# Attention scores from each head's own 32 or 64 partitions, without GpSimd's masked copies of the queries

## The chip, the cores and the metric

The kernel runs on one core of a Trainium2 chip. The metric is the device time of one execution in microseconds, as the median of several. The engines are TensorE (PE in rows of the profile, PEld for its weight loads), VectorE (DVE), ScalarE (ACT), GpSimd (POOL) and SyncE (SP, which only issues DMAs here). SBUF has 128 partitions; a matmul contracts over partitions and writes PSUM, which has eight banks.

## The reference

Two blocks in float32. The first has two layers on 256 latent tokens and 256 context tokens of width 1024: token mixers in four groups (spatial gating A, Fourier mixing B, differential attention C, neighbourhood attention D), then a mixture of 16 experts; the second has feed-forward layers, a recurrent unit and pooling, and is not touched here. What matters is in C and D:

```python
q, k: (tokens, 4 heads, 2 maps, 32)          # group C, normed, rope
s = einsum('bqhmd,bkhmd->bhmqk', q, k) * 32 ** -0.5
a = softmax(s); w = a[:, :, 0] - lam * a[:, :, 1]
out_c = einsum('bhqk,bkhd->bqhd', w, v)
q, k: (tokens, 4 heads, 64)                  # group D, normed
s = q . k * 64 ** -0.5 + bias(-inf outside the window), context keys without bias
out_d = softmax(s) v
```

So a score of C is a product over 32 numbers and one of D over 64.

## The kernel before

One program for five engines, each with its own order of instructions written out by hand and ordered among each other by semaphores. Per layer the mixers run as: input projections (`projection`), transposes of queries and keys of C (`turn_qk(l, 0)`), spatial gating, Fourier, attention C (`attention_c`), transposes of D (`turn_qk(l, 1)`), attention D (`attention_d`), `merge`, then routing and the experts. In layer 0 only, `ada_group` steps (L709, L717: a product of `ada_w` with the conditioning, on four 32-column strips of TensorE, then transposes) stand between these on TensorE.

`qk_t` holds the transposed queries (blocks 0 and 1) and keys (blocks 2 and 3), 128 features on the partitions and tokens along the free dimension. In C a block has two heads with two maps of 32 features each, in D two heads of 64. A full product over 128 partitions would mix these. So GpSimd writes copies of the queries in which all partitions but the head's own are zero (L496 for C, L513 for D: a multiplication by a 0/1 column of `const`, `band_c`, `band_d`) into `q_band`, and TensorE takes the product of that copy with the whole block of keys (L819, L857).

A unit is one query tile of 128 tokens and one head: 16 in layer 0 (four tiles), 8 in layer 1. `keys(q)` gives 512 keys for latent tiles (the first eight units) and 256 for context tiles (the other eight of layer 0). Every engine takes the units in turn. In C, PE in iteration u: four (or two) transposes of the weights of u (L832) into bank 6, the two score products of u + 3 (L819) into banks 2(u % 3) and the next, then the value product of u (L841). VectorE: the weights of u + 1 in four steps (L1775, L1776, L1778 and L1779, the last reads two tensors in SBUF and writes one), then the two maxima of u + 3 (L1763, read from PSUM), and at each new tile a copy of the finished tile (L1768); the next tile's value product waits for that copy, and so does all behind it on PE. ScalarE: the copy of the turned weights (L1346) and the exponentials (L1335). The exponentials of u + 3 free the bank pair.

In D, PE in iteration u: the score of u + 2 (L857), for latent tiles followed by a product that adds the bias `rel_bias` (L861), the transposes of u + 1 (L871), the value product of u (L886). ScalarE has there, besides exponentials (L1359) and copies (L1377), squares and roots for the norm of the outputs, with a table load at each change, and a piece of `w_out` (L354).

GpSimd in a layer, strictly in this order: DMAs of `att` (Fourier tables and the mask) and `rel_bias`, the 8 copies of the first four C units, two more each time a unit's scores are done, the addition of the mask to `rel_bias` (L505, 128 x 2048, SBUF to SBUF), the D copies. PE's `attention_d` waits once for `bias_ready`, which L505 gives. The weights of all stages come by DMA through a ring of six slots of 2 MB; SyncE issues a load when PE has released the slot (`weights_used`).

Of the kernel before, what the change touches and what calls it, by code (L numbers as in the profile page):

```python
# [19 lines left out]
ALU = mybir.AluOpType  # L20
# [3 lines left out]
P = 128  # L24
# [7 lines left out]
HEADS, HEAD = 4, 64  # L32
# [29 lines left out]
CONST = {"ident": P, "slot_row": CAP, "slot_col": 1, "band_c": P // DIFF, "band_d": P // HEAD, "cos": 4 * DIFF, "sin": 4 * DIFF}  # L62
# [15 lines left out]
def lru_pairs():  # L78
# [18 lines left out]
    "c_bands": 16, "d_bands": 16, "c_scores": 32, "c_max": 32, "c_exp": 32, "c_weights": 16, "c_turned": 16, "c_wt": 16, "c_pv": 16, "c_out": 4,  # L97
# [29 lines left out]
def build(nc, dram, out_t):  # L127
    ctx = ExitStack()
    with ctx:
# [5 lines left out]
        def sem(name):  # L135
            if name not in sems:
                sems[name] = ctx.enter_context(nc.semaphore(name))
            return sems[name]
# [30 lines left out]
        def part(lo, hi):  # L169
            return arena[:, lo:hi]  # L170
# [7 lines left out]
        q_band = part(7168, 8192).rearrange("p (b f) -> p b f", b=8)  # L178
# [290 lines left out]
        def _(pool):  # L469
            for l in range(LAYERS):  # L470
# [15 lines left out]
                pool.wait_ge(sem("qk_t_act"), 1 + before("qk_t_act", l))  # L486
                pool.wait_ge(sem("qk_t_dve"), 1 + before("qk_t_dve", l))
                band = const[:, columns(CONST, "band_c")]
                for u, (q, h) in enumerate(units(l)):
                    if u == 0:  # L490
                        pool.wait_ge(sem("qk_turned"), 4 + before("qk_turned", l))
                    if u >= 4:
                        pool.wait_ge(sem("c_scores"), 2 * (u - 3) + before("c_scores", l))
                    for m in range(2):
                        g = 2 * h + m
                        ins = pool.tensor_scalar(q_band[:, 2 * (u % 4) + m, :], qk_t[:, g // 4, P * q:P * q + P],  # L496
                                                 band[:, g % 4:g % 4 + 1], None, ALU.mult)
                    ins.then_inc(sem("c_bands"), 1)

# [6 lines left out]
                pool.wait_ge(sem("qk_t_act"), 3 + before("qk_t_act", l))  # L506
                pool.wait_ge(sem("qk_t_dve"), 3 + before("qk_t_dve", l))
                pool.wait_ge(sem("c_scores"), 2 * len(units(l)) + before("c_scores", l))
                band = const[:, columns(CONST, "band_d")]
                for u, (q, h) in enumerate(units(l)):  # L510
                    if u >= 8:
                        pool.wait_ge(sem("d_scores"), u - 7 + before("d_scores", l))
                    pool.tensor_scalar(q_band[:, u % 8, :], qk_t[:, h // 2, P * q:P * q + P],  # L513
                                       band[:, h % 2:h % 2 + 1], None, ALU.mult).then_inc(sem("d_bands"), 1)
# [154 lines left out]
        def _(pe):  # L669
# [134 lines left out]
            def attention_c(l):  # L804
# [4 lines left out]
                def scores(u):  # L809
# [7 lines left out]
                    pe.wait_ge(sem("c_bands"), u + 1 + before("c_bands", l))  # L817
                    for m in range(2):
                        pe.matmul(ps[:, 2 * (u % 3) + m, 0:width], q_band[:, 2 * (u % 4) + m, :],  # L819
                                  qk_t[:, 2 + (2 * h + m) // 4, lo:lo + width], start=True, stop=True)\  # L820
                            .then_inc(sem("c_scores"), 1)
# [23 lines left out]
            def attention_d(l):  # L845
# [5 lines left out]
                def scores(u):  # L851
                    q, h = todo[u]
                    lo, width = keys(q)
                    if u >= 3:
                        pe.wait_ge(sem("d_exp"), u - 2 + before("d_exp", l))
                    pe.wait_ge(sem("d_bands"), u + 1 + before("d_bands", l))
                    mm = pe.matmul(ps[:, u % 3, 0:width], q_band[:, u % 8, :], qk_t[:, 2 + h // 2, lo:lo + width],  # L857
                                   start=True, stop=q >= 2)
# [1368 lines left out]
def host_constants():  # L2227
# [9 lines left out]
    const["band_c"] = np.kron(np.eye(P // DIFF), np.ones((DIFF, 1)))  # L2237
# [144 lines left out]
```

## Time and profile before

| | us |
|---|---|
| three executions | 2664.91, 2666.49, 2666.72 |
| median | 2666.49 |
| profiled execution | 2663.66 |
| its span, first to last instruction | 2661.9 |
| busy in it: TensorE, VectorE, ScalarE, GpSimd | 2294.2, 1036.2, 810.8, 67.6 |
| mean granted clock of TensorE | 0.967 of full speed |
| DMA: moved, mean rate | 660.17 MB, 248 GB/s |
| layer 0: C from about 179 to 230, D from 242 to 286 | |
| layer 1: C from about 996 to 1034, D from 1037 to 1068 | |

Times in rows are from the start of the span. In the chain of waits each piece lasts from its start until the next piece could begin; in the timeline a row is a group of like instructions, whose durations overlap where TensorE is pipelined, so starts are the safer numbers.
### The profile page before, as it was taken

The page shows a single profiled execution, that of the slowest core. Times are in us where ns is not written, and L with a number is a line of the kernel's source. Part 1 is how long each engine was busy: PE and PEld are TensorE (multiplying, and loading weights), DVE is VectorE, ACT ScalarE, POOL GpSimd, SP SyncE. Part 2 cuts the span into 40 slices and gives each one's busy share as a digit, 9 for nine tenths or more (in the row PEclk, how much of TensorE's full clock was granted, in tenths as well). Part 3 has the DMA queues.
Part 4 walks back from the last instruction along what each step waited for, and adds up shares of the span by engine and source line. Part 5 has one row for each costly group of instructions (what it writes and reads, how often), then busy time and mean ns, then how long its engine had stood idle before and what let it go on. Part 6 is the DMA issues. An engine that isn't in the chain of part 4 may idle for free.

```text
span 2661.9 us, 32502 instructions
## 1 busy us (share of the span) xinstructions
PE 2294.2 (86%) x13947; PEld 1607.4 (60%) x13952; DVE 1036.2 (39%) x1361; ACT 810.8 (30%) x989; POOL 67.6 (3%) x99
## 2 busy tenths in 40 slices
PE   5998888877777897797777779999999989979997
PEld 3855643222222685531111129998999989978997
DVE  4536451000000556410000005557765565555555
ACT  3425321100000346310000004434644354334433
POOL 0023000000000002000000000000000000010000
PEclk8999899999999998799999999999999999999998
DMA  6292256999999230479999993444354434442441
GB/s 269 111 382 120 118 217 281 428 428 429 428 427 429 101 138 0 180 310 428 429 428 428 429 428 157 189 162 175 127 190 184 157 149 186 189 158 97 188 174 68
DMA packets 49840, 660.17 MB, mean 248 GB/s; under 512 B 5616, under 2 KB 7152, under 8 KB 8144
## 3 DMA queue, kind: packets, MB, share of 16 engines
q1 hardware_dynamic: 48640, 653.67, 60.0%
q0 software_dynamic: 1104, 5.11, 0.5%
q8 instruction: 73, 1.20, 0.2%
q14 instruction: 23, 0.19, 0.0%
HBM read 657.71 MB, written 1.05 MB: 247 GB/s over the span
## 4 chain that ended last, share of the span: by engine, by line
PE 58%; DMA 29%; DVE 7%; ACT 4%; issue 1%; SPq 0%; POOL 0%; DVEq 0%; ACTq 0%; POOLq 0%
DMA ring<-in_exp_down 13%; PE ps L680 13%; PE ps L681 13%; PE ps L682 13%; DMA ring<-in_exp_gate 12%; PE ps L997 4%; PE ps L1012 3%; DMA ring<-in_ffn_w 2%; DVE ring_r L361 2%; PE ps L553 2%; ACT ring_r L354 1%; PE ps L1028 1%; PE ps L819 1%; DMA ring<-in_w_in 1%; PE ps L964 1%
## 5 line engine op out<-in xcount | busy, mean ns | idle before, releaser
L997 PE MATMUL ps<-ring,arena 128*64 128x512 f32 (+1 forms) x2048 | 468.3, 602 | 136.2 <-DMA ring<-in_exp_up 64.8
L680 PE MATMUL ps<-h_buf_r,ring_r 128*128 128x256 f32 (+1 forms) x1856 | 539.8, 291 | 16.5 <-DVE h_buf_r L638 12.2
L682 PE MATMUL ps<-h_buf_r,ring_r 128*128 128x256 f32 (+1 forms) x1856 | 537.2, 289 | 0.0
L361 DVE TENSOR_TENSOR ring_r<-ring,ring_r 128x4096 fp32r<-128x4096 f32 (+2 forms) x97 | 406.1, 4192 | 301.3 <-ACT ring_r L354 301.3
L681 PE MATMUL ps<-h_buf_r,ring_r 128*128 128x256 f32 x1696 | 483.0, 285 | 0.0
L997 PEld LDWEIGHTS ps<-ring,arena 128*64 128x64 f32 (+1 forms) x2048 | 129.6, 124 | 473.6 <-issue 294.3
L354 ACT ACTIVATE ring_r<-ring 128x4096 fp32r<-128x4096 f32 (+2 forms) x97 | 332.7, 3434 | 255.1 <-DMA ring<-in_ffn_w 226.4
L680 PEld LDWEIGHTS ps<-h_buf_r,ring_r 128*128 128x128 f32 x1856 | 359.6, 194 | 21.7 <-issue 16.8
L682 PEld LDWEIGHTS ps<-h_buf_r,ring_r 128*128 128x128 f32 x1856 | 359.5, 194 | 3.1
L681 PEld LDWEIGHTS ps<-h_buf_r,ring_r 128*128 128x128 f32 x1696 | 328.5, 194 | 0.2
L681 PE MATMUL ps<-arena_r,ring_r 128*128 128x256 f32 (+1 forms) x944 | 277.8, 294 | 0.0
L1012 PE MATMUL ps<-ring,arena 128*64 128x512 f32 (+1 forms) x1024 | 232.2, 597 | 32.3 <-ACT arena L1444 19.8
L1954 DVE TENSOR_TENSOR arena<-arena,ps 128x512 f32<-128x512 f32 (+1 forms) x32 | 21.9, 683 | 560.9 <-PE ps L997 560.9
L680 PE MATMUL ps<-arena_r,ring_r 128*128 128x256 f32 x784 | 223.5, 285 | 3.4 <-DVE arena_r L1988 1.8
L682 PE MATMUL ps<-arena_r,ring_r 128*128 128x256 f32 x784 | 222.9, 284 | 0.0
L681 PEld LDWEIGHTS ps<-arena_r,ring_r 128*128 128x128 f32 x944 | 182.6, 193 | 3.1
L1012 PEld LDWEIGHTS ps<-ring,arena 128*64 128x64 f32 (+1 forms) x1024 | 62.0, 123 | 181.4 <-issue 118.1
L680 PEld LDWEIGHTS ps<-arena_r,ring_r 128*128 128x128 f32 x784 | 151.5, 193 | 4.5 <-DVE arena_r L1988 2.3
L682 PEld LDWEIGHTS ps<-arena_r,ring_r 128*128 128x128 f32 x784 | 151.5, 193 | 0.0
L1962 DVE COPY arena<-ps 32x512 f32 x32 | 21.9, 686 | 285.9 <-PE ps L1012 285.9
L1444 ACT ACTIVATE arena<-ps 128x512 f32<-128x512 f32 (+1 forms) x32 | 15.7, 490 | 322.8 <-PE ps L1004 322.8
L680 PE MATMUL ps<-ring_r,h_buf_r 128*128 128x512 f32 (+1 forms) x240 | 92.5, 386 | 15.3 <-DVE arena_r L619 15.3
(273 smaller groups left out, 2311.5 us busy)
## 6 DMA issues: line engine op xcount, KB each, us to landing
ring<-in_exp_gate SPq DMA_DIRECT2D x64, 2048.0 KB, 25.4
ring<-in_exp_up SPq DMA_DIRECT2D x64, 2048.0 KB, 25.6
ring<-in_exp_down SPq DMA_DIRECT2D x64, 2048.0 KB, 24.9
ring<-in_ffn_w SPq DMA_DIRECT2D x60, 2048.0 KB, 8.2
ring<-in_ada_w SPq DMA_DIRECT2D x24, 2048.0 KB, 15.2
ring<-in_w_in SPq DMA_DIRECT2D x6, 2048.0 KB, 19.1
ring<-in_ffn_w SPq DMA_DIRECT2D x12, 1024.0 KB, 4.9
ring<-in_lru_w SPq DMA_DIRECT2D x6, 2048.0 KB, 8.3
```

Source lines behind the costliest of these rows:

```text
L354: act.activation(halves(n)[0][:, 0:halved[n]], slot(n)[:, 0:halved[n]], ACT.Copy).then_inc(sem("chunk_lead"), 1)
L361: dve.tensor_tensor(rest, slot(n)[:, 0:halved[n]], lead, ALU.subtract).then_inc(sem("chunk_halved"), 1)
L553: mm = pe.matmul(ps[:, 0, 0:width], mean_w[:, :], squares(i)[:, k, 0:width], start=k == 0, stop=k == KT - 1)
L680: release(pe.matmul(out, a[0], b[0], start=start, stop=False, skip_group_check=True))
L681: pe.matmul(out, a[0], b[1], start=False, stop=False, skip_group_check=True)
L682: return pe.matmul(out, a[1], b[0], start=False, stop=stop, skip_group_check=True)
L819: pe.matmul(ps[:, 2 * (u % 3) + m, 0:width], q_band[:, 2 * (u % 4) + m, :], qk_t[:, 2 + (2 * h + m) // 4, lo:lo + width], start=True, stop ...
L964: mm = pe.matmul(ps[:, j % 6, :], h, one_hot, start=a == 0 and i == 0, stop=a == 1 and i == 1)
L997: mm = pe.matmul(ps[half * m:half * m + m, which, :], xe[:, k, :], slot(n + c)[:, D * (k % 4) + 512 * half:D * (k % 4) + 512 * half + 512] ...
L1012: mm = pe.matmul(ps[half * m:half * m + m, 3, :], hid_t[:, k % 4, k // 4, :], slot(n + c)[:, D * (k % 4) + 512 * half:D * (k % 4) + 512 * ...
L1028: mm = pe.matmul(ps[:, 4 + d % 4, N * s:N * s + N], o[:, g, P * d:P * d + P], scatter[:, s, g, :], start=g == 0, stop=g == 3)
L1954: dve.tensor_tensor(hid, hid, ps[0:2 * m, 1, :], ALU.mult).then_inc(sem("exp_hid"), 1)
```

## The change

Scores read only the head's own partitions: for C the strip `32*(2*(h%2)+m)` to +32 of block `h//2` of the queries and of block `2 + h//2` of the keys, for D the strip `64*(h%2)` to +64. TensorE addresses such a product to the same rows of its array (32x128 at row 0, 32, 64 or 96; 64x128 at row 0 or 64). The two maps of a C unit are on two neighbouring strips, the next head's on the other two. All of GpSimd's copies, their waits, semaphores, buffer and constants are gone. Banks, the order on the other engines and the values computed stay.

```diff
@@ GpSimd, per layer
                 pool.dma_start(rel_bias, dram["rel_bias"][l]).then_inc(sem("rel_bias_loaded"), 16)
 
-                pool.wait_ge(sem("qk_t_act"), 1 + before("qk_t_act", l))
-                pool.wait_ge(sem("qk_t_dve"), 1 + before("qk_t_dve", l))
-                band = const[:, columns(CONST, "band_c")]
-                for u, (q, h) in enumerate(units(l)):
-                    if u == 0:
-                        pool.wait_ge(sem("qk_turned"), 4 + before("qk_turned", l))
-                    if u >= 4:
-                        pool.wait_ge(sem("c_scores"), 2 * (u - 3) + before("c_scores", l))
-                    for m in range(2):
-                        g = 2 * h + m
-                        ins = pool.tensor_scalar(q_band[:, 2 * (u % 4) + m, :], qk_t[:, g // 4, P * q:P * q + P],
-                                                 band[:, g % 4:g % 4 + 1], None, ALU.mult)
-                    ins.then_inc(sem("c_bands"), 1)
-
                 pool.wait_ge(sem("att_loaded"), 16 + before("att_loaded", l))
                 pool.wait_ge(sem("rel_bias_loaded"), 16 + before("rel_bias_loaded", l))
...
                 pool.tensor_tensor(biases, biases, masks, ALU.add).then_inc(sem("bias_ready"), 1)
-                pool.wait_ge(sem("qk_t_act"), 3 + before("qk_t_act", l))
-                pool.wait_ge(sem("qk_t_dve"), 3 + before("qk_t_dve", l))
-                pool.wait_ge(sem("c_scores"), 2 * len(units(l)) + before("c_scores", l))
-                band = const[:, columns(CONST, "band_d")]
-                for u, (q, h) in enumerate(units(l)):
-                    if u >= 8:
-                        pool.wait_ge(sem("d_scores"), u - 7 + before("d_scores", l))
-                    pool.tensor_scalar(q_band[:, u % 8, :], qk_t[:, h // 2, P * q:P * q + P],
-                                       band[:, h % 2:h % 2 + 1], None, ALU.mult).then_inc(sem("d_bands"), 1)
@@ TensorE, attention_c, scores(u)
-                    pe.wait_ge(sem("c_bands"), u + 1 + before("c_bands", l))
                     for m in range(2):
-                        pe.matmul(ps[:, 2 * (u % 3) + m, 0:width], q_band[:, 2 * (u % 4) + m, :],
-                                  qk_t[:, 2 + (2 * h + m) // 4, lo:lo + width], start=True, stop=True)\
-                            .then_inc(sem("c_scores"), 1)
+                        b, own = h // 2, slice(DIFF * (2 * (h % 2) + m), DIFF * (2 * (h % 2) + m) + DIFF)
+                        pe.matmul(ps[:, 2 * (u % 3) + m, 0:width], qk_t[own, b, P * q:P * q + P],
+                                  qk_t[own, 2 + b, lo:lo + width], start=True, stop=True).then_inc(sem("c_scores"), 1)
@@ TensorE, attention_d, scores(u)
-                    pe.wait_ge(sem("d_bands"), u + 1 + before("d_bands", l))
-                    mm = pe.matmul(ps[:, u % 3, 0:width], q_band[:, u % 8, :], qk_t[:, 2 + h // 2, lo:lo + width],
-                                   start=True, stop=q >= 2)
+                    own = slice(HEAD * (h % 2), HEAD * (h % 2) + HEAD)
+                    mm = pe.matmul(ps[:, u % 3, 0:width], qk_t[own, h // 2, P * q:P * q + P],
+                                   qk_t[own, 2 + h // 2, lo:lo + width], start=True, stop=q >= 2)
```

Where GpSimd's instructions stand. Before, layer 0, from the load of `rel_bias` on (L496 C copies, L505 the mask addition, L513 D copies; lines are those of the kernel before):

```order
L484 DMA h_buf<-in_rel_bias 128x2048
L496 ISA
L496 TENSOR_SCALAR arena<-arena,const 128x128 [waits qk_turned,qk_t_dve,qk_t_act]
L496 TENSOR_SCALAR arena<-arena,const 128x128 x7
L496 TENSOR_SCALAR arena<-arena,const 128x128 [waits c_scores]
...
L505 TENSOR_TENSOR h_buf<-h_buf 128x2048 [waits rel_bias_loaded,att_loaded]
L513 TENSOR_SCALAR arena<-arena,const 128x128 [waits c_scores,qk_t_dve,qk_t_act]
L513 TENSOR_SCALAR arena<-arena,const 128x128 x7
L513 TENSOR_SCALAR arena<-arena,const 128x128 [waits d_scores] x8
```

After the change, GpSimd in layer 0 and on to layer 1 (line numbers are those of the changed kernel: L490 is the mask addition, L481 to L483 the three loads):

```order
L482 DMA h_buf<-in_att 128x1280
L483 DMA h_buf<-in_rel_bias 128x2048
L490 ISA
L490 TENSOR_TENSOR h_buf<-h_buf 128x2048 [waits rel_bias_loaded,att_loaded]
L476 DMA rows<-in_rows 128x384 [waits moe_added,sgu_done,qk_ready]
L477 DMA arena<-in_sgu_t 128x512
L481 DMA h_buf<-in_att 128x256 [waits proj_done]
```

The mask addition L505 stood behind 32 C copies, of which 24 (in pairs, the first of a pair) wait for `c_scores`; as L490 it stands behind the loads and waits for them alone.

TensorE at the start of stretch C in layer 0, before (L819 scores, L832 transposes, L841 value product):

```order
L819 MATMUL ps<-arena 128x512 [waits c_bands,qk_t_dve,qk_t_act]
L819 MATMUL ps<-arena 128x512
L819 MATMUL ps<-arena 128x512 [waits c_bands]
L819 MATMUL ps<-arena 128x512
L819 MATMUL ps<-arena 128x512 [waits c_bands,fourier_read]
L819 MATMUL ps<-arena 128x512
L832 MATMUL ps<-const,arena 128x128 [waits c_weights]
L832 MATMUL ps<-const,arena 128x128 x3
L819 MATMUL ps<-arena 128x512 [waits c_bands,c_exp]
L819 MATMUL ps<-arena 128x512
L841 MATMUL ps<-arena 128x64 [waits c_wt]
```

and in the changed kernel (L795 scores, L807 transposes, L816 value product):

```order
L795 MATMUL ps<-arena 128x512 [waits qk_t_dve,qk_t_act]
L795 MATMUL ps<-arena 128x512 x3
L795 MATMUL ps<-arena 128x512 [waits fourier_read]
L795 MATMUL ps<-arena 128x512
L807 MATMUL ps<-const,arena 128x128 [waits c_weights]
L807 MATMUL ps<-const,arena 128x128 x3
L795 MATMUL ps<-arena 128x512 [waits c_exp]
L795 MATMUL ps<-arena 128x512
L816 MATMUL ps<-arena 128x64 [waits c_wt]
L816 MATMUL ps<-arena 128x64 x3
L807 MATMUL ps<-const,arena 128x128 [waits c_wt,c_weights]
```

No instruction of TensorE has moved; the waits for `c_bands` are gone, and with them the only link from GpSimd to stretch C.

## Rows read from the trace of the kernel before

**Rows 1.** Chain of waits, layer 0, one steady unit: start us, us, engine and line.
```profile
193.34 0.44 PE ps L832 x4
193.78 1.72 PE ps L819 x4
195.50 0.84 PE ps L841 x8
```

**Rows 2.** Timeline, VectorE: start us, us, engine, line, operation, names, shapes, count [idle].
```profile
1013.76 1.27 DVE L1763 TENSOR_REDUCE small<-ps 128x1 f32<-128x512 f32 x2
1014.96 0.15 DVE L1775 RECIPROCAL small<-small 128x2 f32<-128x2 f32 x1
1016.53 0.68 DVE L1763 TENSOR_REDUCE small<-ps 128x1 f32<-128x512 f32 x1
...
217.59 0.74 DVE L1763 TENSOR_REDUCE small<-ps 128x1 f32<-128x256 f32 x2
218.26 0.15 DVE L1775 RECIPROCAL small<-small 128x2 f32<-128x2 f32 x1
219.43 0.75 DVE L1763 TENSOR_REDUCE small<-ps 128x1 f32<-128x256 f32 x2
```

**Rows 3.** Line L1779 (min/median/max ns); timeline: L1779 in layer 1, L505.
```profile
L1779 DVE SCALAR_TENSOR_TENSOR arena<-arena,small x16: 483/751/4608, 186.3 to 227.0; 128x512 f32<-128x512 f32 x8, 128x256 f32<-128x256 f32 x8
...
1008.96 4.88 DVE L1779 SCALAR_TENSOR_TENSOR arena<-arena,small 128x512 f32<-128x512 f32 x1
...
212.82 4.56 POOL L505 TENSOR_TENSOR h_buf<-h_buf 128x2048 f32<-128x2048 f32 x1
```

**Rows 4.** GpSimd's queue in the timeline, and DMA issues of two stretches.
```profile
149.01 0.54 POOL L484 DMA_DIRECT2D h_buf<-in_rel_bias  x1
...
h_buf<-in_rel_bias POOLq DMA_DIRECT2D x1, 1024.0 KB, 17.4
...
988.21 0.54 POOL L484 DMA_DIRECT2D h_buf<-in_rel_bias  x1
...
h_buf<-in_rel_bias POOLq DMA_DIRECT2D x1, 1024.0 KB, 6.4
```

**Rows 5.** Timeline, VectorE: the first maximum of each layer's stretch C.
```profile
180.52 1.48 DVE L1763 TENSOR_REDUCE small<-ps 128x1 f32<-128x512 f32 x2 [0.55 <-PE ps L819]
...
997.07 0.69 DVE L1763 TENSOR_REDUCE small<-ps 128x1 f32<-128x512 f32 x1 [0.17 <-PE ps L819]
```

**Rows 6.** Timeline, TensorE: full tiles, then 128x32 column strips (L709), twice.
```profile
150.15 1.89 PE L788 MATMUL ps<-arena 128*128 128x256 f32 x8
...
151.98 7.07 PE L709 MATMUL ps<-ring,cond 128*32 128x512 f32 x64
...
163.72 7.07 PE L776 MATMUL ps<-arena,h_buf 128*128 128x256 f32 x32
...
170.72 5.36 PE L709 MATMUL ps<-ring,cond 128*32 128x512 f32 x48
```

**Rows 7.** Timeline, VectorE: the copies L1768 that the counts end at.
```profile
224.73 0.41 DVE L1768 COPY arena<-ps 128x256 f32<-128x256 f32 x1
...
1024.59 0.41 DVE L1768 COPY arena<-ps 128x256 f32<-128x256 f32 x1
```

**Rows 8.** Window (busy us of PE, PEld, DVE, ACT, POOL; clock; DMA), timeline.
```profile
1004.00:1009.00 5.00, 5.00 (x21) 3.22 (x20) 3.42 (x8) 2.15 (x5) 1.55 (x3) 0.66 0.00 0
...
1004.23 3.12 PE L819 MATMUL ps<-arena 128*128 128x512 f32 x4
```

**Rows 9.** Window, layer 0, stretch D (columns as in rows 8).
```profile
242.00:286.00 44.00, 35.94 (x200) 26.94 (x202) 27.14 (x68) 31.36 (x61) 4.82 (x8) 0.88 0.22 93
```

**Rows 10.** Timeline, layer 1: last copy ahead of stretch D, its first score.
```profile
1035.93 0.69 DVE L1753 COPY arena<-ps 128x512 f32<-128x512 f32 x1 [1.00 <-PE ps L799]
...
1036.83 1.10 PE L857 MATMUL ps<-arena 128*128 128x512 f32 x2 [0.94 <-POOL arena L513]
```

**Rows 11.** Waits of the DMA queue: us in total, times, longest.
```profile
SPq L440 <- PE ps L997: 561.5, 120, 44.3
```

More of the change, by code:

```diff
@@ L60 @@
 ROWS_W = sum(ROWS.values())
-CONST = {"ident": P, "slot_row": CAP, "slot_col": 1, "band_c": P // DIFF, "band_d": P // HEAD, "cos": 4 * DIFF, "sin": 4 * DIFF}
+CONST = {"ident": P, "slot_row": CAP, "slot_col": 1, "cos": 4 * DIFF, "sin": 4 * DIFF}
 CONST_W = sum(CONST.values())
@@ L96 @@
     "fourier_uv": 4, "uv_ready": 4, "fourier_done": 4, "fourier_read": 2,
-    "c_bands": 16, "d_bands": 16, "c_scores": 32, "c_max": 32, "c_exp": 32, "c_weights": 16, "c_turned": 16, "c_wt": 16, "c_pv": 16, "c_out": 4,
+    "c_scores": 32, "c_max": 32, "c_exp": 32, "c_weights": 16, "c_turned": 16, "c_wt": 16, "c_pv": 16, "c_out": 4,
     "d_scores": 16, "d_max": 16, "d_exp": 16, "d_turned": 16, "d_wt": 16, "d_pv": 16, "d_out": 16,
@@ L177, in build @@
         expo = part(4096, 7168).rearrange("p (b f) -> p b f", b=6)
-        q_band = part(7168, 8192).rearrange("p (b f) -> p b f", b=8)
         qk_d = part(8192, 10240).rearrange("p (t f) -> p t f", t=4)
@@ L2235, in host_constants @@
     }
-    const["band_c"] = np.kron(np.eye(P // DIFF), np.ones((DIFF, 1)))
-    const["band_d"] = np.kron(np.eye(P // HEAD), np.ones((HEAD, 1)))
     half = DIFF // 2
```

## The prediction

> **What bounds the kernel now.** Outside the two attention stretches nothing in the kernel is touched, so I read those, one per layer, and first the chain of waits there. In layer 0's first attention (the "C" heads, `attention_c`) the chain lies on TensorE: per unit (one head of one query tile, 512 keys) four transposes 0.44 us, the two score products 1.72, the eight passes of the value product 0.84, together 3.00 [rows 1]. GpSimd's copies are nowhere in it. Then VectorE, at two places where score results lay ready: from the first of a unit's two maxima to the first step of the weights 1013.76 to 1014.96, 1.20 us, and on to the next unit's maxima at 1016.53, so 1.57 for the four steps of weights and 2.77 in all. With 256 keys the same rows give 0.67, 1.17 and 1.84 [rows 2]. **VectorE is only 0.23 us per unit behind TensorE: it is the next bound, and it caps what shorter scores can give.** Third, the longest single item on either chain: the step L1779 takes 0.483 or 0.751 us, but once per layer 4.61 and 4.88, when GpSimd's addition of the mask (L505, 4.56 us) is running [rows 3]. The order of GpSimd's program puts L505 behind all the copies of stretch C, so it falls into the middle of VectorE's work.
>
> **Part 1: the mask addition moves.** With no copies ahead of it, L505 starts when its loads land: in layer 0 149.01 + 17.4 = 166.4 us, in layer 1 988.21 + 6.4 = 994.6 [rows 4]. It then runs until about 171.0 and 999.2. In layer 0 the first maximum is taken at 180.52: cover enough [rows 4, 5]. In layer 1 VectorE does one copy out of PSUM and maxima over PSUM from 997.07 on, and its first step on two SBUF tensors comes after 1002 [rows 5]. I take nothing for a collision there; the upper bound is what L505 still has to run at 996.2, 3.0 us (a rival below). Gain: 4.61 − 0.48 = 4.13 and 4.88 − 0.75 = 4.13, **8.3 us**, both on the chain. The Trainium skill ("SBUF — State Buffer", section "SBUF: two separate sides") says that GpSimd and a VectorE operation with two SBUF inputs exclude each other for the whole instruction; the long L1779 agrees with it, and so does taking nothing for operations that read PSUM.
>
> **Part 2: scores in row tiles.** Each product is two passes of 512 columns, 0.43 us each [rows 1]. Fewer rows do not shorten a pass (I assume; it streams as many columns), so the gain can only be overlap. The two products of a unit now use different 32-row strips and different PSUM banks. The trace has no row strips side by side, but column strips: 64 passes L709 on 128x32 strips, 512 wide, take 7.07 us, 0.11 each against 0.43 of a score pass, so four ran at once [rows 6, 1]. Bounds: no overlap (1.72 per unit) and full overlap of a pair (0.86). I take 0.86, since the nearest row shows overlap between strips for the same type and width.
>
> **Part 3: changes of tile shape.** TensorE now changes between 128 rows and 32 or 64 rows twice per unit. Price: L788's 8 passes to L709 are 1.83 us, L776's 32 passes of the same width to L709 7.00; the 24 between them cost 5.17, 0.2155 each, which leaves 0.105 for the change [rows 6]. Two per unit are 0.2 us; bounds 0 (hidden) and 0.2. TensorE's unit in stretch C becomes 3.00 − 0.86 + 0.2 = 2.34, under VectorE's 2.77: the changes are hidden and **VectorE is the bound.**
>
> **Part 4: stretch C anew, by VectorE's clock.** The maxima of the first three units no longer wait for passes of 0.86 us each. I count from the first maximum (180.52; 997.07) to the copy L1768 that gates the last value products (224.73 in layer 0, ahead of unit 12's; 1024.59 in layer 1, ahead of unit 4's) [rows 5, 7]. Behind that copy only transposes, value products and ScalarE copies follow, unchanged.
> Layer 0: maxima of 8 units at 1.20 and 8 at 0.67 = 14.96; weights of units 0 to 13, 8 x 1.57 + 6 x 1.17 = 19.58; two earlier copies at about 0.33; sum 35.2, so 215.7. Layer 1: 8 x 1.20 + 6 x 1.57 = 19.0, so 1016.1.
> New waits: (a) TensorE ends the first scores about 0.6 us after the first maximum begins, and the first weights end 3 x 1.20 + 1.57 after it, so TensorE now idles some 4.5 us. Before, in layer 1, the pause in this place was followed by 5 us at a granted 0.66 of full speed, part of them at 1.2 GHz, and the four score passes took 3.12 us there [rows 8]. I expect one such stretch at 1.2 GHz at each start: transposes 0.88 and scores 1.72 instead of 0.44 and 0.86, against VectorE's 1.57 of cover: 2.6 + 0.3 − 1.57 = 1.3 us per layer (bounds 0 and 3). (b) Where a new query tile begins, the copy, value product, transposes and scores run in series: 0.41 + 0.84 + 0.44 + 0.43 (two passes of 256) + 0.2 + some 0.3 of hand-overs = 2.6 us, against VectorE's own 0.33 + 1.57: it waits 0.7. At the next, with 256 keys in all of it, 0.41 + 0.42 + 0.22 + 0.43 + 0.2 + 0.3 = 2.0 against 1.5: 0.5. Both lie inside layer 0's count, none in layer 1's.
> Copy L1768 at 215.7 + 1.3 + 1.2 = 218.2 instead of 224.73: **−6.5 us**. Layer 1: 1016.1 + 1.3 = 1017.4 instead of 1024.59: **−7.2 us**. Part 1 is contained in both.
>
> **Part 5: the second attention ("D").** One product per unit, nothing beside it to overlap with, so no gain in scores. The chain names GpSimd's copies once, at layer 1's first D score (0.94 us), but the copy L1753 of the transposed keys ends at 1035.93 + 0.69 = 1036.62 and the score starts at 1036.83 [rows 10]: the real wait is for VectorE, gain 0. In layer 0 `ada_group` lies ahead. The cost is 24 units x 0.2 = 4.8 us of shape changes. In layer 0's D neither engine is busy throughout (TensorE 35.94 and ScalarE 31.36 of 44 us [rows 9]), now one is late and now the other, so I take half, **+2.4 us** (bounds 0 and 4.8).
>
> **What follows later.** Stretches behind are chains of engines, and the expert weights are requested when TensorE frees a slot (120 waits, 561.5 us [rows 11]), so the experts' DMA-bound part starts earlier by the same amount and keeps its length. GpSimd's other work is not in any chain.
>
> **Sum.** −6.5 − 7.2 + 2.4 = −11.3 us. The profiled execution took 2663.66 (span 2661.9), 2.83 under the median of the three runs, 2666.49; the change of 11.3 is set against both alike: 2652.4 profiled, **2655.2 us** as a median. A difference under 0.2% (5.3 us) can't be told from none.
>
> **Rivals.**
> (A) *No overlap of row strips.* TensorE stays the bound with 3.00 + 0.2 per unit. Of the count 13 and 5 units pay 0.2; 8.3 − 3.6 − 2.4 = 2.3 us gained: 2664. For: no row shows row strips side by side. Against: L709 [rows 6]. Chance 0.10.
> (A') *Passes start strictly in program order.* The two passes of one product sit on one strip, one behind the other; then a pair takes three steps, 1.29 us, a unit 3.00 − 0.43 + 0.2 = 2.77, level with VectorE, and each of the four waits of part 4 grows by 0.43: 2655.2 + 1.7 = 2656.9. For: the trace has no row of it. Against: L709 also has two passes per product and strip, and runs four at once. Chance 0.05. The Trainium skill ("TensorE: Matmul & The Clock Gate", section "The mechanism" of its part 3) states this rule: matmuls start and end in program order.
> (B) *Slower: the granted clock stays low.* TensorE now pauses in every unit and fills 32 of 128 rows; if 1.2 GHz holds through stretch C, a unit is 0.88 + 1.72 + 1.68 + 0.2 = 4.5 us against 3.00. Layer 0: 8 x 1.5 + 8 x 0.3; layer 1: 8 x 1.5 less the 3 us that its low stretches cost already; + 2.4 of D, − 8.3: about +17, 2684. It decides against the change once more than six or seven 512-key units run low (each 4.5 − 2.77 = 1.7 us against 11.3). For: rows 8. Against: low stretches there lasted one or two units. Chance 0.06.
> (C) *The mask addition collides elsewhere.* Layer 1's first copy and maxima wait until 999.2, 3 us: 2658. For: rows 3. Against: those read PSUM. Chance 0.10.
> (D) *Half the gain is lost later*, to falls of the clock at new places (in one such stretch four score passes stood at 3.12 us [rows 8], which are 1.72 of the chain elsewhere) or to a transfer: 2661. Chance 0.07.
> My forecast has 0.62.
>
> **How the numbers follow.** Fast end: no low clock at the starts (−2.6) and shape changes hidden (−2.4) and low stretches of before gone (−2): 2648. Slow end: A, 2664. B alone lies outside, with parts of A. Faster by over 0.2%, below 2661.2: the forecast, A', C, and part of D: 0.80. Slower: B, 0.05. Same: the rest, 0.15.
>
> **What would show it.** Score passes that start in pairs, about 0.86 us per unit; VectorE without idle in stretch C, unit to unit 2.8 us; L1779 never above 0.8; L505 at 166 and 995 us; D units about 0.2 longer where TensorE is late. Score passes at 1.72 per unit mean A; a granted clock near 0.5 across stretch C means B; a copy L1746 of 3 us means C. Wrong beyond the range: a gain above 18 us, which would need VectorE to be shorter than counted.

## The result, and the profile after

The changed kernel took **2696.76 us** (median of 2692.03, 2695.79, 2697.74 and 2702.26), against 2666.6 us of the kernel before on the same chip: a ratio of 1.0115, 95% interval 1.0095 to 1.0135. It is 30 us **slower**, where 11 us less was forecast. Its runs spread over 10 us, those of before over 2. The profiled execution took 2692.03 us, with a span of 2690.2.

Start with TensorE's clock in the attention stretches of the changed kernel. The view is the table by windows, with the granted clock in the column PEclk; the first four windows are in layer 0 and the last two in layer 1.

```profile
core 0: us, PE busy (x) PEld busy (x) DVE busy (x) ACT busy (x) POOL busy (x), PEclk, DMA share, GB/s
180.60:185.40 4.80, 0.79 (x4) 0.00 (x0) 4.65 (x10) 3.98 (x10) 0.00 (x0) 1.00 0.97 410
185.40:250.20 64.80, 58.51 (x220) 38.73 (x224) 34.64 (x93) 25.70 (x76) 0.00 (x0) 0.50 0.28 120
250.20:284.40 34.20, 31.47 (x186) 17.35 (x178) 16.60 (x42) 22.54 (x40) 0.00 (x0) 1.00 0.45 184
284.40:311.70 27.30, 25.60 (x95) 16.30 (x98) 10.74 (x28) 9.55 (x23) 0.00 (x0) 0.50 0.04 9
1021.10:1025.10 4.00, 0.86 (x7) 0.04 (x2) 3.91 (x8) 3.18 (x6) 1.88 (x1) 1.00 0.00 0
1025.10:1066.00 40.90, 35.12 (x128) 24.31 (x128) 19.68 (x44) 15.23 (x38) 0.00 (x0) 0.50 0.00 0
```

In layer 0 the clock is at 1.2 GHz (0.50) for 65 us without a break, all of stretch C, and for 27 us more from near the end of stretch D on; in layer 1 for 41 us. The same view of the kernel before has a mean of 0.94 over its stretch C of layer 0 (180.5 to 233 us) and 0.87 over that of layer 1 (997 to 1036): dips of a few us each.

The timeline of TensorE at the start of stretch C in layer 0, changed kernel (L795 scores, L807 transposes, L816 value product; they answer to L819, L832 and L841 in [rows 1]):

```profile
179.41 1.99 PE L795 MATMUL ps<-arena 32*128 32x512 f32 x12
...
185.95 1.11 PE L807 MATMUL ps<-const,arena 128*128 128x128 f32 x4 [4.56 <-DVE arena L1754]
186.99 2.08 PE L795 MATMUL ps<-arena 32*128 32x512 f32 x4
189.00 1.97 PE L816 MATMUL ps<-arena 128*128 128x64 f32 x8
190.76 1.06 PE L807 MATMUL ps<-const,arena 128*128 128x128 f32 x4
...
195.52 1.06 PE L807 MATMUL ps<-const,arena 128*128 128x128 f32 x4
```

Three things are to be seen. Twelve score passes start and end within 1.99 us, where before they took 5.32: strips overlap. Then TensorE idles 4.56 us. From there a unit lasts 190.76 − 185.95 = 4.81 us and then 195.52 − 190.76 = 4.76, TensorE has no gap in it, and every pass takes about twice as long as at full clock. VectorE, which was to be the bound, waits in each unit (timeline of VectorE, changed kernel):

```profile
193.86 1.29 DVE L1738 TENSOR_REDUCE small<-ps 128x1 f32<-128x512 f32 x2 [1.89 <-PE ps L795]
```

The mask addition did what was expected. It starts at 166.49 us, and the step that it used to delay (L1754, formerly L1779) has no long case left (timeline of GpSimd, and groups by shape of VectorE in stretch C of layer 0, to set beside [rows 3]):

```profile
166.49 4.51 POOL L490 TENSOR_TENSOR h_buf<-h_buf 128x2048 f32<-128x2048 f32 x1 [17.03 <-DMA h_buf<-in_rel_bias]
```
```profile
L1754 DVE SCALAR_TENSOR_TENSOR arena<-arena,small 128x512 f32<-128x512 f32 x8 | 6.0, 751 | 0.3
```

And the two copies that the prediction used as marks, L1743 now, beside the first maxima of their stretch (timeline of VectorE; the first two rows are layer 0, the others layer 1):

```profile
180.64 3.68 DVE L1738 TENSOR_REDUCE small<-ps 128x1 f32<-128x512 f32 x6 [0.74 <-PE ps L795]
...
237.67 0.41 DVE L1743 COPY arena<-ps 128x256 f32<-128x256 f32 x1
...
1021.14 3.68 DVE L1738 TENSOR_REDUCE small<-ps 128x1 f32<-128x512 f32 x6 [0.36 <-PE ps L795]
...
1049.85 0.42 DVE L1743 COPY arena<-ps 128x256 f32<-128x256 f32 x1
```

From first maximum to copy, layer 0 took 57.0 us (before 44.2, forecast 37.7) and layer 1 28.7 (before 27.5, forecast 20.3) [rows 5, 7]. Layer 1's stretch begins 24.1 us later than before, so most of the loss (28.3 us by the spans) had been made in layer 0 by then. Of these 24.1 us, 16.2 had been lost when stretch D began (first score of D at 257.82 us, before at 241.58) and 5.0 more within stretch D (48.9 us from its first score to the next `ada_group`, before 43.9). In layer 1 the same two steps are 5.5 and 1.1 us.

One execution of the kernel with strips in stretch C alone (3021 us, below) was disturbed and stands outside all comparisons.

### The profile page after: what moved, and what is told of

It reads as the page before. It is cut to its first block, busy times and chain, and to the rows that moved or that the text cites. A ratio compares the mean times of both kernels' runs of the same rounds, so it can differ in the third digit from the quotient of the medians.

```text
span 2690.2 us, 32387 instructions
## 1 busy us (share of the span) xinstructions
PE 2330.7 (87%) x13947; PEld 1622.4 (60%) x13952; DVE 1026.7 (38%) x1361; ACT 811.2 (30%) x989; POOL 24.7 (1%) x27
## 4 chain that ended last, share of the span: by engine, by line
PE 59%; DMA 29%; DVE 6%; ACT 4%; issue 1%; SPq 0%; DVEq 0%; ACTq 0%
DMA ring<-in_exp_down 13%; PE ps L656 13%; PE ps L657 13%; PE ps L658 13%; DMA ring<-in_exp_gate 12%; PE ps L972 4%; PE ps L987 3%; PE ps L529 2%; DVE ring_r L360 2%; DMA ring<-in_ffn_w 2%; PE ps L816 1%; PE ps L1003 1%; ACT ring_r L353 1%; PE ps L795 1%; DMA ring<-in_w_in 1%; PE ps L685 1%
## 5 line engine op out<-in xcount | busy, mean ns | idle before, releaser
L1419 ACT ACTIVATE arena<-ps 128x512 f32<-128x512 f32 (+1 forms) x32 | 15.7, 491 | 322.9 <-PE ps L979 322.9
## 6 DMA issues: line engine op xcount, KB each, us to landing
ring<-in_ada_w SPq DMA_DIRECT2D x24, 2048.0 KB, 15.2
```

## Experiments

Two questions: which half of the change brings the loss, and what holds the clock down. Theory R (in some expectations S, S2 or, in its last form, H): the strip passes do (they use 32 or 64 of 128 rows). Rival P: the longer pause does. In the diffs, `filler(n)` issues n products of `qk_t[:, 0, 0:P]` with `qk_t[:, 2, 0:N]` (full rows, 256 columns) into a PSUM bank that nobody reads then.

### The mask addition alone, and each half alone

First, the kernel before with the mask addition ahead of all query copies.

```diff
...
+                pool.tensor_tensor(biases, biases, masks, ALU.add).then_inc(sem("bias_ready"), 1)
                 for u, (q, h) in enumerate(units(l)):
...
-                pool.tensor_tensor(biases, biases, masks, ALU.add).then_inc(sem("bias_ready"), 1)
```

> The kernel before with one edit: GpSimd adds the mask to rel_bias ahead of its query copies for stretch C, not behind them. All passes stay on full rows. Theory T (part 1 of the prediction): VectorE's L1779, which waited for the shared port in stretch C, loses its long outliers, 4.1 us a layer, so about 8.3 us less than before, near 2658 us, and the granted clock stays as it was. Rival: GpSimd's first copies now start behind the addition (4.6 us), and the first scores of stretch C wait for them, so that the gain is given back: 2662 to 2671 us.

Measured: 2664.42 us against 2667.35, ratio 0.9984 (0.9975 to 0.9993), so about 4 us less by the ratio. Both were right in part. No long L1779 is left (eight at 751 ns, eight at 484 in layer 0). But in layer 1 the first copies now stood behind the addition, and TensorE waited for them (groups by shape, 985 to 1037 us):

```profile
L819 PE MATMUL ps<-arena 128*128 128x512 f32 x32 | 18.0, 703 | 4.6 <-POOL arena L502 4.6
```

Then the strips in stretch C alone (D keeps its copies), and in stretch D alone (C keeps its copies, the addition behind them). The edits are the two halves of the change; the kernel with strips in C alone has the moved mask addition too.

> Only stretch C reads strips of 32 partitions; stretch D keeps GpSimd's masked copies and full rows. In the changed kernel the landmarks fell back by some 16 us in stretch C of layer 0, some 7 us in stretch D of layer 0 and some 6 us in layer 1. If the loss belongs to the 32-row passes of stretch C (theory S: while they run, the granted clock stays at 0.5), this kernel keeps the 22 us of stretch C and is 18 to 26 us slower than before, with the clock at 0.5 from about 185 to 230 us. If the 64-row passes of stretch D are to blame as much as those of C, it is 10 to 15 us slower. If the loss needs both, under 5 us.

> Only stretch D reads strips of 64 partitions; stretch C keeps GpSimd's masked copies and full rows, and the mask addition stays behind them. Theory S2 (64-row passes lower the granted clock too, in proportion to rows in use): the clock falls to 0.5 in stretch D and the kernel is 5 to 9 us slower than before. Rival (the low clock in stretch D of the changed kernel was an effect of what C left behind, or of the times at which ada_group 4 fell): the clock stays near that of before, and the time is within 0 to +3 us of before (part 5 of the prediction said +2.4).

Measured: C alone 2684.14 us, ratio 1.0057 (1.0042 to 1.0073); D alone 2684.86, ratio 1.0059 (1.0039 to 1.0080). By the ratios the halves cost 15.2 and 15.7 us, together as much as the change (0.0057 + 0.0059 against 0.0115). That fits the case of halves that are to blame alike, where 10 to 15 us had been expected of C alone; theory S had 18 to 26 for it, and theory S2 5 to 9 for D alone. C alone includes what the moved addition gives, so its strips cost more than 15.2. The equal sums do not show that the changed kernel loses half in D: in its profiled execution, the fastest of four, the two stretches D were 5.0 and 1.1 us longer than before, in that of D alone, the second slowest of five, 13.4 and 11.4. The profile of C alone was taken again:

> The kernel with strips in stretch C alone once more, for its profile: the first one was of a disturbed execution (3021 us, the whole of it at 0.75). Theory R: the clock is at 0.5 from about 185 us to the end of stretch C, and in stretch D as in the kernel before. Rival (the low clock of stretch D in the changed kernel came from stretch C): nothing to see in D here or in the kernel with strips in D alone, which has shown 48 us of it.

This one took 2683.2 us (by windows, layer 0: stretch C, then from its end to the middle of stretch D):

```profile
185.00:249.00 64.00, 57.65 (x216) 38.54 (x220) 34.49 (x93) 25.73 (x76) 1.37 (x3) 0.50 0.28 119
250.00:286.00 36.00, 30.12 (x196) 19.17 (x188) 17.75 (x46) 26.18 (x43) 7.10 (x12) 1.00 0.43 175
```

D alone, by windows and by TensorE's timeline where the clock falls:

```profile
243.60:256.70 13.10, 12.28 (x53) 6.70 (x53) 5.56 (x13) 8.85 (x16) 0.00 (x0) 1.00 0.79 340
256.70:304.50 47.80, 46.84 (x160) 32.50 (x164) 21.86 (x57) 22.93 (x46) 0.00 (x0) 0.50 0.00 1
1058.80:1106.60 47.80, 43.72 (x139) 31.01 (x138) 21.07 (x47) 29.34 (x48) 0.00 (x0) 0.50 0.00 1
```
```profile
256.64 1.11 PE L861 MATMUL ps<-const,arena 128*128 128x128 f32 x4 [0.82 <-ACT arena L1349]
```

Strips in C lower the clock in C and leave D as it was; strips in D lower it in D, in both layers. As it was does not mean 1.0 throughout: the kernel before, full rows in every score, has a low stretch of 10.2 us in its own stretch D of layer 0 (window below, kernel before), where TensorE waited up to 2.6 us for ScalarE, and C alone has one of 10.2 us at the same units.

```profile
271.00:281.00 10.00, 7.41 (x30) 6.12 (x28) 6.56 (x13) 2.86 (x10) 0.00 (x0) 0.50 0.00 0
```

In D alone, from 243.6 us to the fall, TensorE waited once, 0.82 us; in the kernel before it waited 0.37 and 1.50 us in the same place and the clock stayed up. A long pause is not needed.

### The pause

> The changed kernel with nine full-row passes of 256 columns, whose results nobody reads, right behind the first three units' scores, where TensorE idled 4.56 us. Theory P (the pause brings the clock down, and it then stays down): without the pause the clock stays at 1.0 through most of stretch C, and the time falls by 15 us or more against the changed kernel, to about 2680 or less. Theory S (the 32-row passes themselves): the clock falls again within some units, as no full-row passes come between, and the time stays above 2690.

```diff
                 for u in range(3):
                     scores(u)
+                filler(9)
```

Measured: 2680.54 us, ratio 1.0052 (1.0036 to 1.0067) where the changed kernel has 1.0115: about half of the loss is gone, as P said. But the profile shows what R said too: the clock holds for five units and falls behind the next pause, 1.93 us long.

```profile
190.82 1.10 PE L821 MATMUL ps<-arena 128*128 128x64 f32 x8 [0.26 <-ACT arena L1326]
...
193.60 1.10 PE L821 MATMUL ps<-arena 128*128 128x64 f32 x8 [0.17 <-ACT arena L1326]
...
200.91 1.08 PE L821 MATMUL ps<-arena 128*128 128x64 f32 x8 [1.93 <-DVE arena L1748]
```
```profile
203.10:237.20 34.10, 30.14 (x121) 21.98 (x122) 17.83 (x56) 12.83 (x43) 0.00 (x0) 0.50 0.02 10
```

While it held, a unit took 193.60 − 190.82 = 2.78 us, with VectorE never idle: the pace that part 4 had worked out (2.77).

> The changed kernel with the nine full-row passes behind the first scores and one more full-row pass of 256 columns at the end of each unit of stretch C (0.43 us at full clock). With the first nine alone the clock fell at 203 us, not at 185, and the kernel was 13 us slower than before. Theory R (strip passes, which use part of the rows, do not keep the clock up, full-row passes do): the clock stays at 1.0 in stretch C of layer 0, the units take 2.8 us, stretch D still falls as it did, and the time is 2672 to 2678. Rival (it is the idle time, of which little is left): no further change, 2680.

```diff
+                filler(9)
...
                     mm.then_inc(sem("c_pv"), 1)
+                    filler(1)
```

Measured: 2687.97 us (eight runs, 2680.98 to 2703.89), ratio 1.0083 (1.0058 to 1.0109). Neither theory's figure, and a spread of 23 us. In layer 1 the clock held through all of stretch C; in layer 0 it fell behind a pause of 1.80 us at 200 us, and the full-row product of 256 columns in each unit did not bring it back:

```profile
200.30:251.50 51.20, 47.18 (x168) 33.69 (x172) 19.93 (x60) 14.78 (x47) 0.00 (x0) 0.50 0.05 19
...
1030.00:1084.00 54.00, 45.47 (x246) 29.92 (x244) 32.98 (x71) 34.98 (x68) 1.88 (x1) 1.00 0.00 1
```

Now the pause without strips. VectorE gets four more maxima over SBUF ahead of its first weights:

```diff
+                for i in range(4):
+                    dve.tensor_reduce(d_max[:, i:i + 1], qk_t[:, 0, :], AX, ALU.max)
                 weights(0)
```

> The kernel before, all passes on full rows, with four extra maxima of 512 columns on VectorE ahead of its first unit of each stretch C (they read SBUF and nobody uses what they give), so that TensorE's first pause grows from 2.4 to about 4.8 us, as in the changed kernel. Rival P (the pause alone brings the clock down for long): the clock falls to 0.5 near 185 us and stays there for tens of us, and the time rises by 10 us or more. Theory R (strips): one dip of 3.4 us, and 2 x 2.4 us plus the dips: 2672 to 2675.

Measured, one execution: 2671.07 us beside 2667.74 of before, 1 us under what theory R had. The pause is 4.73 us, longer than the changed kernel's 4.56, and the dip is 6.8 us, twice the expected 3.4. By the timeline, and by windows:

```profile
188.41 1.11 PE L832 MATMUL ps<-const,arena 128*128 128x128 f32 x4 [4.73 <-DVE arena L1779]
```
```profile
186.50:193.30 6.80, 4.89 (x12) 2.83 (x12) 4.24 (x11) 1.38 (x3) 0.26 (x1) 0.50 1.01 429
```

**Behind the same pause the clock is low for 6.8 us with full rows, and for 65 us with strips.** P alone falls: the low stretch starts at the pause, and what follows decides how long it lasts.

### Rows and the clock, without any wait

Blocks of passes that wait for nobody, put ahead of stretch C of layer 0. For n rows on the strips that start at r:

```diff
+                    for i in range(count):
+                        r = starts[i % len(starts)]
+                        pe.matmul(ps[:, r // 32, 0:N], qk_t[r:r + n, 0, 0:P], qk_t[r:r + n, 2, 0:N], start=True, stop=True)
```

> The kernel before with blocks of TensorE passes of 128x256 whose results nobody reads, ahead of stretch C of layer 0, one behind the other without a wait: full rows (20 us) before and after each of: 64 rows; 32 rows; 32 rows on two strips in turn; 32 rows on four strips in turn; 64 rows on two strips in turn. Theory R: with 64 or 32 rows of one strip the clock falls to 0.5 inside the block and comes back in the full-row block behind it; with strips in turn that overlap to cover all 128 rows it stays at 1.0, and two strips of 32 behave as 64 rows do. Rival (rows do not matter, only idle time): the clock stays at 1.0 through all blocks, since TensorE never waits. The overlap: a pass of 256 columns takes 0.43 us alone, 0.22 on two strips in turn, 0.11 on four.

By windows: 64 rows; 32 rows; full rows again; 32 rows on two strips; on four strips; 64 rows on two strips.

```profile
202.00:229.00 27.00, 27.00 (x126) 23.20 (x125) 0.00 (x0) 0.00 (x0) 0.00 (x0) 1.00 0.07 28
...
254.00:301.00 47.00, 47.00 (x111) 36.57 (x111) 0.00 (x0) 0.00 (x0) 0.00 (x0) 0.50 0.00 0
305.00:323.00 18.00, 18.00 (x85) 15.86 (x84) 0.00 (x0) 0.00 (x0) 0.00 (x0) 1.00 0.00 1
325.00:351.00 26.00, 26.00 (x244) 23.10 (x242) 0.00 (x0) 0.00 (x0) 0.00 (x0) 1.00 0.01 1
373.00:400.00 27.00, 27.00 (x504) 25.64 (x504) 0.00 (x0) 0.00 (x0) 0.00 (x0) 1.00 0.01 2
422.00:449.00 27.00, 27.00 (x254) 24.23 (x252) 0.00 (x0) 0.00 (x0) 0.00 (x0) 1.00 0.01 1
```

TensorE is busy in all of every window. With 32 rows of one strip the clock fell 3.4 us into the block and came back in the full-row block, so "idle time alone" falls. That 64 rows of one strip held it at 1.0 was not as R expected. The overlap is complete (timeline of TensorE; 64 rows, then 32 rows on two strips and on four):

```profile
201.29 27.89 PE L828 MATMUL ps<-arena 64*128 64x256 f32 x128
...
324.02 27.90 PE L838 MATMUL ps<-arena 32*128 32x256 f32 x256
...
372.76 27.91 PE L843 MATMUL ps<-arena 32*128 32x256 f32 x512
```

The same time holds 128, 256 or 512 passes.

Next, the real mixture of passes: 16 units each of stretch C and of stretch D, on full rows and on strips, between blocks of full-row passes.

> The kernel before with blocks of TensorE work ahead of stretch C of layer 0 that waits for nobody: 16 units of stretch C's passes (four transposes, two scores of 512 keys, four value passes) with scores on full rows, then with scores on strips of 32; 16 units of stretch D's passes (four transposes, one score of 512 keys, the bias pass, four value passes) with the score on full rows, then on 64; 20 us of full-row passes of 256 columns between them. The dense run of 32-row passes brought the clock down, dense 64-row passes did not, but stretch D with 64-row scores did. Theory R (the rows in use count, together with the thin passes around them): the clock stays at 1.0 in both full-row patterns and falls to 0.5 within both strip patterns though TensorE never waits. Rival (strips lower the clock only together with waits for other engines): it stays at 1.0 in all four. Then the overlap alone: a unit of stretch C on strips takes 2.2 us against 2.9.

By windows: C on full rows, C on strips, D on full rows, D on 64 rows.

```profile
200.24:248.24 48.00, 48.00 (x257) 32.69 (x256) 0.00 (x0) 0.00 (x0) 0.00 (x0) 1.00 0.07 31
269.01:309.58 40.57, 40.57 (x258) 25.74 (x256) 0.00 (x0) 0.00 (x0) 0.00 (x0) 1.00 0.00 1
330.35:371.52 41.17, 41.17 (x257) 32.69 (x256) 0.00 (x0) 0.00 (x0) 0.00 (x0) 1.00 0.00 1
392.30:439.69 47.39, 47.39 (x258) 31.75 (x256) 0.00 (x0) 0.00 (x0) 0.00 (x0) 1.00 0.00 1
```

R missed here, and its rival held: from a full clock, without waits, none of these four patterns brings the clock down. The windows also give the price of a unit at full clock: C 3.00 and 2.54 us (2.9 and 2.2 had been expected), D 2.57 and 2.96. So a pair of shape changes costs 2.96 − 2.57 = **0.39 us**, and in C 2.54 − (3.00 − 0.86) = 0.40; part 3 had 0.2.

That left one reading: in these mixtures the strips do not push the clock down so much as fail to bring it back. The same patterns, each now behind 40 products on 32 rows that bring the clock to 0.5 first:

> The same blocks of unit patterns as in the run of unit blocks, none of which brought the clock down when TensorE came to them from dense full-row passes and never waited. Here each pattern comes behind 40 dense passes on 32 rows (17 us or more), which bring the clock to 0.5 first; a last pattern is 96 dense passes on 64 rows. Theory H (strip passes do not bring a fallen clock back, full-row passes do): the clock returns to 1.0 within some 3 to 10 us of the full-row patterns of stretches C and D, and only in the dense full-row block behind the strip patterns, so that 16 units of stretch C on strips take some 75 us (4.76 each, as in the changed kernel) and not 41. Rival (any dense work without waits brings it back, and in the changed kernel the waits kept it down): it returns within 10 us in all of them.

By windows: C on full rows, C on strips; D on full rows, D on 64 rows; 64-row passes back to back; the last window is the full-row block behind those.

```profile
234.00:279.00 45.00, 45.00 (x241) 30.65 (x241) 0.00 (x0) 0.00 (x0) 0.00 (x0) 1.00 0.00 1
...
331.00:407.00 76.00, 76.00 (x256) 46.48 (x255) 0.00 (x0) 0.00 (x0) 0.00 (x0) 0.50 0.00 0
...
463.00:502.00 39.00, 39.00 (x246) 31.06 (x245) 0.00 (x0) 0.00 (x0) 0.00 (x0) 1.00 0.00 1
...
553.00:643.00 90.00, 90.00 (x257) 57.20 (x255) 0.00 (x0) 0.00 (x0) 0.00 (x0) 0.50 0.00 0
...
697.00:779.00 82.00, 82.00 (x193) 63.56 (x193) 0.00 (x0) 0.00 (x0) 0.00 (x0) 0.50 0.00 0
784.00:803.00 19.00, 19.00 (x86) 16.00 (x85) 0.54 (x1) 0.00 (x0) 0.00 (x0) 1.00 0.00 1
```

From the low clock, full-row units are back at 1.0 within 4 us of their start (230.5, and 459.8 us). Units of C on strips stay at 0.5 for all 76 us, units of D for 90, and so do even 82 us of 64-row passes without a gap, although the same passes had held a full clock in the run of row blocks. Each came back in the full-row block behind it, as the last window shows for the 64-row passes. The strip unit of C takes 4.76 us here (16 in the 76.2 us from 331.17 to 407.38), with no other engine at work: the changed kernel's 4.76. One thing differs besides rows in the uniform blocks: passes on one strip write one PSUM bank, full-row passes four in turn. The unit patterns write the same banks on full rows and on strips, and in the pattern of D no two scores overlap either, so there only the rows of one product are left as the difference.

### A kernel that beats both

What was good in the change is the moved mask addition. The copies stay, and the addition (`add_mask`, with its two waits) goes behind those of the first four units:

```diff
                 for u, (q, h) in enumerate(units(l)):
+                    if u == 4:
+                        add_mask()
                     if u >= 4:
                         pool.wait_ge(sem("c_scores"), 2 * (u - 3) + before("c_scores", l))
```

> The kernel before, full rows throughout, with GpSimd's mask addition put behind its copies for the first four units of stretch C. With the addition ahead of all copies the kernel gained 4 us: layer 0 lost its stall of 4.1 us, and layer 1 began stretch C 6.2 us later, since its first copies waited for the addition. Theory: with the four copies first, layer 1 keeps its start and both layers lose the stall: about 8 us less than before, 0.997. Rival: the addition now runs beside VectorE's first weights of the stretch (L1779 and its like) and stalls them there, for no gain at all.

Measured: **2657.10 us** against 2667.12, ratio 0.9957 (0.9943 to 0.9971), 10 us faster than before (8 to 15 by the interval). In layer 1 the first copies no longer wait for the addition, and no long case of the former L1779 is left in either layer (groups by shape, 985 to 1037 us; the step is L1783 here):

```profile
L1783 DVE SCALAR_TENSOR_TENSOR arena<-arena,small 128x512 f32<-128x512 f32 x8 | 6.0, 751 | 0.3
```

> The kernel with the mask addition behind the first four units' copies, which took 2657 us (0.9957 of before), and five full-row passes of 256 columns, whose results nobody reads, in TensorE's pause of 2.4 us at the start of each stretch C. Theory: the pause is what brings the dip of 3.4 us that followed it in layer 0 (188 us) and layer 1 (1004 us), so without it the dips go and 1.3 to 1.7 us a layer come back, 2654 us. Rival: the dips move to another place within the stretch and nothing changes, 2657.

```diff
                 for u in range(3):
                     scores(u)
+                filler(5)
```

Measured: **2653.49 us** against 2668.21, ratio 0.9945 (0.9931 to 0.9958). In layer 0 the dip behind the pause is gone, as expected (first row: the kernel without filler; then this one). In layer 1 the clock fell at a later place instead, and for 17 us, where the kernel without filler had 0.90 from 1020 to 1037:

```profile
188.50:191.90 3.40, 3.40 (x7) 1.51 (x6) 1.70 (x3) 1.30 (x3) 0.19 (x1) 0.50 1.02 434
...
187.00:224.00 37.00, 32.64 (x191) 24.14 (x190) 33.83 (x92) 23.08 (x70) 11.35 (x19) 1.00 0.49 206
1019.70:1036.70 17.00, 14.54 (x51) 11.20 (x52) 2.99 (x6) 2.90 (x7) 4.67 (x8) 0.50 0.00 1
```

No score of this kernel runs on a strip. TensorE had value products of 64 columns, transposes and waits of 0.7 and 1.1 us there, and its next scores, of 512 columns, started at 1032.32, 4 us before the clock was back. So a long low stretch is not the mark of strips alone.

The two intervals overlap, so this kernel is faster than the one before, but not shown to be faster than the one without filler. A remedy for stretch D on strips was not tried.

## Why the prediction was wrong

**Part 1 (mask addition, −8.3 us): right.** The long L1779 is gone, and the addition alone, well placed, gave 10 us. It was the only part of the forecast gain that reached the time. Rival C did not happen: in layer 1 GpSimd added from 1018.49 to 1022.99 us, and the copy L1721 at 1020.09 took 0.69 us, as L1746 did before, and the six maxima behind it 3.68, as in layer 0.

**Part 2 (strips overlap, 0.86 for 1.72): right.** The blocks show complete overlap. Rival A is out, and so is A', which had a pair of products at 1.29 us. The Trainium skill ("TensorE: Matmul & The Clock Gate", section "The mechanism") has matmuls start and end in program order; whatever the order is at the level of single passes, it costs nothing here: 256 passes on two strips took 27.90 us and 128 on one 27.89.

**Part 3 (0.2 us a unit for shape changes): half of what it is.** 0.39 to 0.40 at full clock. The 0.105 was worked out from a change between full rows and column strips of 128x32; a change to row strips and back costs twice what the two changes were put at. The Trainium skill ("TensorEngine Tiling (Array Packing)", section "Key Properties") says that a change of tiling mode drains TensorE, without a price; the measured one stands above. In stretch C it would still have been hidden (2.54 against VectorE's 2.77).

**Part 4 (the pace of stretch C): right for a full clock, and the changed kernel had none there after the pause.** 2.78 us against 2.77 in the kernel with the pause filled. The step that failed is wait (a): "I expect one such stretch at 1.2 GHz at each start ... 1.3 us per layer (bounds 0 and 3)". The pause came as forecast (4.56 us for "some 4.5"), the low clock came as forecast, and then it did not end with the unit: 65 us in layer 0, 41 in layer 1. The count from first maximum to copy took 57.0 and 28.7 us where 37.7 and 20.3 were forecast. I had taken the length of a dip from [rows 8], where full-row scores of 512 columns followed; there the clock came back. Behind the changed passes it did not, and no row of before has strips of rows. Two signs were there all the same: the same pause of 2.42 us in layer 0 had no dip behind it (the clock was 1.00 from 186 to 219 us), so a pause did not fix what followed; and the 0.88 of [rows 9] holds the low stretch of 10.2 us over some four units, longer than any in stretch C.

**Part 5 (D, +2.4 us): too small.** D alone cost 15.7 us, 13 more than that. Up to 24 x 0.39 = 9.4 us of it can be shape changes; the rest I put down to the clock, low for 48 us in each layer in its profile. In the profiled execution of the changed kernel both stretches D together were 6.1 us longer.

**Rival B was the case**, put at 0.06 with 2684 us. Its unit of 4.5 us is 4.76 (it priced shape changes at 0.2, and at full clock they are 0.4). Its part for C, 14.4 + 9 − 8.3 = 15.1 us, stands beside 15.2 for C alone, though by layers it was otherwise: 12.8 and 1.2 us by the counts of the changed kernel, where B has 10.3 and 4.9. It kept D at +2.4, and adding the 13 that D alone cost beyond that gives 2697; that this meets the measured 2696.76 is in part luck, since the profiled execution (2692.03) has less in D. Against B I held that "low stretches there lasted one or two units"; those were stretches of another kind of work. Rival B deserved a chance like that of the forecast, since the change altered two things that rows of before could not price: the pause and the rows in use.

## What to carry to other kernels

Before work is moved to row strips, ask what brings TensorE's clock back after a pause: where only strips mixed with short passes followed here, a fall that lasted 7 us with full rows lasted the whole stretch and doubled every pass in it. Price a change from full rows to row strips and back at 0.4 us, and check that the strips run beside each other; alone they save nothing. And when an edit bundles a moved instruction with a rewritten one, try the move by itself: here it held all of the gain, and it wanted a place behind the first copies, not the first place.

## What the runs showed of the hardware

The granted clock depends on its own past: the same passes, without any gap, ran at 1.0 for 27 us when they came to a full clock (64 rows, run of row blocks) and at 0.5 for 82 us when they came to a low one. The Trainium skill ("TensorE: Matmul & The Clock Gate", section "What's actually happening") says that the clock follows how busy TensorE has been recently. Busy as the trace counts it is not enough: TensorE was busy in all of those 82 us. The values do not explain it: scores with copies three quarters of which are zeros brought the clock back in the kernel before ([rows 8], 1.00 again at 1008.2 us). Nor do the columns, since full-row and strip scores use all 128. What differed between the paired unit patterns was the rows in use. Rows are not the whole of it: value products of 64 columns and transposes with short waits, all on full rows, stood at 0.5 for most of 17 us in the last kernel above. Which of columns per pass, transposes and waits counts there was not tried.

Most kernels with strips also spread more from run to run (10 us in the changed kernel, 18 in D alone, 23 with both fillers, against 2 to 9 of before), but C alone did not: 1.4 us over four executions. That a small difference in timing decides whether a fall comes early or late in a stretch would fit this; it is not shown, as only one execution of each has a profile.
